# A two-layer decoder trunk on one core: second softmax group's query and key slabs as 512-column products over both parts of x

## The chip, the core and the metric

One NeuronCore of a Trainium2 chip. The metric is the device time of one execution of the whole program in microseconds, the lower the better.

## What is computed

Two layers of a causal decoder trunk for 256 tokens of width 1024, in 32-bit floats. Layer 0 mixes the normed rows by two head groups, A (gated linear recurrence) and B (block-sparse softmax attention); with 256 tokens every past block is selected, so B is plain causal attention with a rotation of the first 32 dimensions of each head:

```python
h = jnp.einsum('bsd,de->bse', xn, w_in)
aq, af, ai, bq, bk, bv, z = jnp.split(h, splits, axis=-1)
ob = moba_attention(rotary(heads(bq), pos, ROPE_DIM, ROPE_THETA),
                    rotary(heads(bk), pos, ROPE_DIM, ROPE_THETA), heads(bv))
y = jnp.concatenate([oa, ob], axis=-1) * jax.nn.silu(z)
x = x + jnp.einsum('bse,ed->bsd', y, w_out)
```

Layer 1 does the same with two other groups (C, D), and cross attention to 256 memory rows follows each layer. Most of the work is products of the 256 rows with weights of 1024 rows.

## The kernel before

**Split numbers.** Products run on TensorE in a reduced 32-bit format. To keep the precision, each operand is split into a rounded part (hi) and a rest (lo), and three of the four products are summed: w_hi·x_hi, w_hi·x_lo, w_lo·x_hi. x stands transposed in `xT`, whose two parts lie side by side.

**Slabs and quarters.** Weights come in 2 MB slabs, in the order of the list `SLABS` (line 50): stage, part, kind, group. Each slab is cut in four quarters of 128x1024. For each quarter, ScalarE (ACT) rounds the raw weights to w_hi (`ahead`, line 518, instruction L530), VectorE (DVE) subtracts to w_lo (`ahead`, line 1124, L1130), and TensorE (PE) multiplies. A ring of four quarters holds w_hi and w_lo, so `ahead(n, q)`, which prepares quarter 4n + q + 3, waits until the quarter four places back has been used (`quarter_used`). The raw slabs alternate between two buffers; SyncE starts a slab's transfer when the slab two places back has been split.

**Kinds.** An F quarter (`quarter_f`, line 1832, L1848 to L1850) makes for each of eight k three matmuls of 256 columns into one half of a PSUM bank; two quarters share a bank. An X quarter (`quarter_x`, line 1854, L1863 to L1866) makes for each k one matmul of 512 columns, w_hi with both parts of x side by side, and one of 256, w_lo with x_hi: it fills a whole bank, and the two halves have to be added afterwards. Before the change only the gate slabs (z) are X. T quarters (line 1872) have the rows of x as the stationary operand.

**Banks and turns.** Four PSUM banks serve all slabs, as two pairs. `TURN` (line 77) counts: a slab of kind F or T takes one turn, one of kind X two (first and second half of its quarters). A turn's pair is its number modulo 2. `take_bank` (line 1826) lets PE into a bank only when the turn two before has released it:

```python
def bank(n, u, half=0):
    return proj[2 * ((TURN[n] + half) % 2) + u]
def take_bank(n, u, half=0):
    before = (TURN[n] + half) // 2
    if before >= 1:
        pe.wait_ge(free_of(n, u, half), before)
```

**Who releases.** For F and T slabs ACT copies the bank out (`copy_bank`, line 589, L591) and releases. For a z half ACT copies the first 256 columns of both banks (`z_half`, line 579, L586), DVE adds the other 256 (`sum_z`, line 1180, L1185) and DVE releases.

**The stage.** Group 1 of B is `stage_b(1)` on each engine (PE line 2123, ACT line 738, DVE line 1485); the order of the work on each is written out by hand. Its slabs before the change, with their turns: z of group 0 (X, turns 13 and 14), q (F, 15), k (F, 16), v (T, 17), z (X, 18 and 19).
- PE: q quarters 0 and 1; the transposes of group 0's probabilities (`turn_probs_b`, L2109); q quarter 2; group 0's values (`out_b`, L2101); q quarter 3; k; v; first z quarter; the scores (L2144, L2146), which wait for `q_ready`, `k_ready` and `y_ready`; the other z quarters.
- ACT: the copies of the transposed probabilities (`turned_probs`, L779); `ahead(q, 0)`; `z_half` for group 0's second z half; the SiLU of z (`silu`, L576, with a table load); then further `ahead` calls between the copies of q and k. `turn_rows_packed` (line 728) copies the 32 rotated rows of each head into `packed` (L735, twice) and the bank into W (L591). `y_high(2)` (L601) rounds the gated output of group 0.
- DVE: `ahead(q, 0)`; `sum_z` for that z half; `ahead`; the gated output of group 0 (`gated_b`, line 1465, L1470); `ahead`; the rotation of q and of k (`rope_moba`, line 1420, L1425 to L1433).

Of the kernel before, what the change touches and what calls it, by code (L numbers as in the profile page):

```python
# [52 lines left out]
for _g in range(2):  # L53
    SLABS += [("B", "q", "F", _g), ("B", "k", "F", _g), ("B", "v", "T", _g), ("B", "z", "X", _g)]
# [36 lines left out]
def hybrid_trunk(nc, I, out):  # L91
    with ExitStack() as ctx:
# [136 lines left out]
        o_rstd = sem("o_rstd")  # L229
        q_rows = sem("q_rows_copied")  # L230
# [89 lines left out]
        def z_sum(n):  # L320

            if SLABS[n][0] == "C":
                return att[:, :, 0:S]
            return zs[:]

# [191 lines left out]
        def _(act):  # L517
# [210 lines left out]
            def turn_rows_packed(n, u, w, s):  # L728

                filled(act, n, u)  # L730
                if w == 0 and u == 0:
                    act.wait_ge(k_ready, SLABS[n][3])
                for h in range(2):
                    a = 64 * u + 32 * h
                    act.activation(packed[a:a + 32, 2 * w, :], bank(n, u)[0:32, S * h:S * h + S], ACT.Copy)  # L735
                copy_bank(n, u, W[:, w, 512 * u:512 * u + 512], s)

            def stage_b(g):
# [7 lines left out]
                turn_rows_packed(q, 0, 0, q_rows)  # L746
                ahead(q, 3)
                if g:
                    y_high(2)
                ahead(k, 0)  # L750
                turn_rows_packed(q, 1, 0, q_rows)
                ahead(k, 1)
                if g == 0:
                    act.preload_act_table_set("natural_log_exp_and_others")
                    rstd_a(1)
                ahead(k, 2)
                turn_rows_packed(k, 0, 1, k_rows)
                ahead(k, 3)
                if g == 0:
                    y_high(1)  # L760
                ahead(v, 0)
                turn_rows_packed(k, 1, 1, k_rows)
                ahead(v, 1)
# [359 lines left out]
        def _(dve):  # L1123
# [55 lines left out]

            def sum_z(n, half):  # L1180
# [5 lines left out]
                dve.drain().then_inc(free_of(n, 0, half), 1)  # L1186
                dve.nop().then_inc(free_of(n, 1, half), 1)
# [247 lines left out]

            def softmax_max(i, h, moba):
# [48 lines left out]
            def stage_b(g):  # L1485
# [8 lines left out]
                if g == 0:  # L1494
                    mem_turned(0)
                ahead(q, 3)
                if g == 0:
                    mem_turned(1)
                if g:
                    gated_b(0)  # L1500
                ahead(k, 0)
                ahead(k, 1)
                if g == 0:
                    gated_a(1)
                ahead(k, 2)
                rope_moba(0, q_rows, q_ready, 2 * g + 2, k, 3)
                ahead(v, 0)
                rope_moba(1, k_rows, k_ready, 2 * g + 2, v, 1)
                ahead(v, 2)
# [311 lines left out]
        def _(pe):  # L1821
# [32 lines left out]
            def quarter_x(n, q):  # L1854
# [7 lines left out]
                for k in range(KC - 1):  # L1862
                    pe.matmul(both, wh[:, k, :], xT[:, :, k, :], start=(k == 0), stop=False)  # L1863
                    pe.matmul(dst[:, 0:S], wl[:, k, :], xT_hi[:, k, :], start=False, stop=False)  # L1864
                pe.matmul(dst[:, 0:S], wl[:, KC - 1, :], xT_hi[:, KC - 1, :], start=False, stop=False)  # L1865
                pe.matmul(both, wh[:, KC - 1, :], xT[:, :, KC - 1, :], start=False, stop=True).then_inc(quarter_used, 1)  # L1866

            def slab_x(n, qs=range(4)):
                for q in qs:
                    quarter_x(n, q)  # L1870
# [252 lines left out]
            def stage_b(g):  # L2123
# [7 lines left out]
                else:  # L2131
                    slab_f(q, [0, 1])
                    turn_probs_b(0)
                    slab_f(q, [2])
                    out_b(0)
                    slab_f(q, [3])
                    slab_f(k)
# [234 lines left out]
```

## Time and profile before

| | us |
|---|---|
| median of 3 runs | 584.78 (584.31 to 584.93) |
| the profiled execution | 585.06 |
| its span, first to last instruction | 583.2 |
| PE busy | 573.4 (98%) |
| DVE busy | 426.0 (73%) |
| ACT busy | 390.6 (67%) |
| mean granted TensorE clock | 0.999 |

Busy time is the union of an engine's instructions. The ends of matmuls are modelled and overlap the next one, so the pace of a stream of matmuls is read from the starts, not from the durations. PEld is TensorE's loading of the stationary operand, which runs beside the matmuls. Idle time of an engine counts only where the chain of waits goes through it.

### The profile page before, as it was taken

How to read it: one execution, taken by the hardware profiler on the slowest of the kernel's cores; microseconds unless marked ns; L12 is line 12 of the kernel's file. 1: busy time of each engine (PE TensorE's matmuls, PEld its weight loads, DVE VectorE, ACT ScalarE, POOL GpSimd, SP SyncE). 2: the span in 40 equal slices, each digit the busy share in tenths (PEclk: the TensorE clock that was granted, in tenths of full speed). 3: DMA queues.
4: the chain of work that ended last, by engine and by line, in shares of the span. 5: the costliest groups of instructions: out<-in, count | busy, mean ns of one | idle time of the engine just before them, and what ended most of it. 6: DMA issues, size and time to landing. Idle time of an engine off the chain costs nothing.

```text
span 583.2 us, 9261 instructions
## 1 busy us (share of the span) xinstructions
PE 573.4 (98%) x3612; PEld 518.5 (89%) x3612; DVE 426.0 (73%) x662; ACT 390.6 (67%) x597; POOL 73.7 (13%) x77
## 2 busy tenths in 40 slices
PE   7999999999999999999999999999999999999995
PEld 6999989899899888889988999999889988888985
DVE  6879779686756874567557865799997974876663
ACT  6863784578458575657666847969759837566754
POOL 4330005026401000100000001102110200100002
PEclk9999999999999999999999999999999999999999
DMA  9757355556824833565345545326544563356201
GB/s 294 242 182 234 92 198 188 175 158 173 238 83 148 286 145 144 178 221 180 145 144 169 193 151 194 121 113 218 215 146 145 162 247 142 112 207 227 97 1 73
DMA packets 51855, 98.86 MB, mean 170 GB/s; under 512 B 1732, under 2 KB 7140, under 8 KB 51812
## 3 DMA queue, kind: packets, MB, share of 16 engines
q1 hardware_dynamic: 50628, 96.95, 49.2%
q0 software_dynamic: 1024, 1.05, 0.7%
q8 instruction: 29, 0.48, 0.3%
q10 hardware_dynamic: 160, 0.27, 0.1%
q14 instruction: 14, 0.11, 0.1%
HBM read 96.16 MB, written 1.05 MB: 167 GB/s over the span
## 4 chain that ended last, share of the span: by engine, by line
PE 97%; DVE 1%; DMA 1%; ACT 0%; issue 0%; SPq 0%; DVEq 0%; ACTq 0%
PE proj L1848 12%; PE proj L1850 11%; PE proj L1849 11%; PE proj L1885 11%; PE proj L1887 11%; PE proj L1886 11%; PE proj L1863 9%; PE proj L1864 5%; PE head L2101 4%; PE proj L1866 1%; PE head L2177 1%; PE head L2284 1%; PE head L1945 1%; DMA x_residual<-in_x_dram 1%; PE proj L1865 1%; PE head L2078 1%
## 5 line engine op out<-in xcount | busy, mean ns | idle before, releaser
L1130 DVE TENSOR_TENSOR w_lo<-raw_weights,w_hi 128x1024 fp32r<-128x1024 f32 x174 | 223.9, 1300 | 99.1 <-ACT w_hi L530 96.5
L530 ACT ACTIVATE w_hi<-raw_weights 128x1024 fp32r<-128x1024 f32 x174 | 182.2, 1056 | 111.5 <-PE proj L1887 49.2
L1848 PE MATMUL proj<-xT,w_hi 128*128 128x256 f32 x496 | 142.4, 287 | 0.0
L1850 PE MATMUL proj<-xT,w_lo 128*128 128x256 f32 x496 | 140.4, 283 | 0.0
L1849 PE MATMUL proj<-xT,w_hi 128*128 128x256 f32 x496 | 140.3, 283 | 0.0
L1848 PEld LDWEIGHTS proj<-xT,w_hi 128*128 128x128 f32 x496 | 95.0, 192 | 0.8 <-DVEq L1186 0.4
L1849 PEld LDWEIGHTS proj<-xT,w_hi 128*128 128x128 f32 x496 | 95.1, 192 | 0.5
L1850 PEld LDWEIGHTS proj<-xT,w_lo 128*128 128x128 f32 x496 | 95.0, 192 | 0.0
L1863 PE MATMUL proj<-xT,w_hi 128*128 128x512 f32 x224 | 81.1, 401 | 0.0
L1885 PE MATMUL proj<-w_hi,y_hi 128*128 128x512 f32 x176 | 69.4, 395 | 0.0
L1887 PE MATMUL proj<-w_lo,y_hi 128*128 128x512 f32 x176 | 68.6, 390 | 0.0
L1886 PE MATMUL proj<-w_hi,y_lo 128*128 128x512 f32 x176 | 68.5, 389 | 0.0
L1864 PE MATMUL proj<-xT,w_lo 128*128 128x256 f32 x224 | 62.7, 280 | 0.0
L1863 PEld LDWEIGHTS proj<-xT,w_hi 128*128 128x128 f32 x224 | 42.1, 188 | 8.8
L1864 PEld LDWEIGHTS proj<-xT,w_lo 128*128 128x128 f32 x224 | 42.3, 189 | 0.8
L443 POOL TENSOR_TENSOR y_lo<-work,y_hi 128x1024 fp32r<-128x1024 f32 x6 | 15.7, 2609 | 193.5 <-ACT y_hi L601 193.5
L1887 PEld LDWEIGHTS proj<-w_lo,y_hi 128*128 128x128 f32 x176 | 33.0, 188 | 7.0
L1886 PEld LDWEIGHTS proj<-w_hi,y_lo 128*128 128x128 f32 x176 | 33.1, 188 | 6.7
L1885 PEld LDWEIGHTS proj<-w_hi,y_hi 128*128 128x128 f32 x176 | 33.1, 188 | 6.7
L1885 PE MATMUL proj<-w_hi,xT 128*128 128x512 f32 x96 | 37.4, 390 | 0.0
L1886 PE MATMUL proj<-w_hi,xT 128*128 128x512 f32 x96 | 37.4, 390 | 0.0
L1887 PE MATMUL proj<-w_lo,xT 128*128 128x512 f32 x96 | 37.3, 389 | 0.0
(313 smaller groups left out, 901.5 us busy)
## 6 DMA issues: line engine op xcount, KB each, us to landing
raw_weights<-in_ev_w_in_dram SPq DMA_DIRECT2D x15, 2048.0 KB, 9.7
raw_weights<-in_od_w_in_dram SPq DMA_DIRECT2D x12, 2048.0 KB, 8.0
raw_weights<-in_ev_w_out_dram SPq DMA_DIRECT2D x4, 2048.0 KB, 7.7
raw_weights<-in_xa_wkv_dram SPq DMA_DIRECT2D x4, 2048.0 KB, 8.3
raw_weights<-in_od_w_out_dram SPq DMA_DIRECT2D x4, 2048.0 KB, 7.7
raw_weights<-in_xa_wq_dram SPq DMA_DIRECT2D x2, 2048.0 KB, 9.0
raw_weights<-in_xa_wo_dram SPq DMA_DIRECT2D x2, 2048.0 KB, 8.4
x_residual<-in_x_dram SPq DMA_DIRECT2D x2, 512.0 KB, 4.1
```

The lines of the kernel that those rows point to most:

```text
L443: pool.tensor_tensor(y_lo[:, 4 * G:4 * G + 4, :], y_src(i), y_hi[:, 4 * G:4 * G + 4, :].bitcast(F32), ALU.subtract).then_inc(y_lo_ready, 1)
L530: act.activation(ring_quarter(w_hi, n, q), raw_quarter(n, q), ACT.Copy).then_inc(hi_ready, 1)
L1130: dve.tensor_tensor(ring_quarter(w_lo, n, q), raw_quarter(n, q), ring_quarter(w_hi, n, q).bitcast(F32), ALU.subtract).then_inc(lo_ready, 1)
L1848: pe.matmul(dst, wh[:, k, :], x_hi[:, k, :], start=(k == 0), stop=False)
L1849: pe.matmul(dst, wh[:, k, :], x_lo[:, k, :], start=False, stop=False)
L1850: last = pe.matmul(dst, wl[:, k, :], x_hi[:, k, :], start=False, stop=(k == KC - 1))
L1863: pe.matmul(both, wh[:, k, :], xT[:, :, k, :], start=(k == 0), stop=False)
L1864: pe.matmul(dst[:, 0:S], wl[:, k, :], xT_hi[:, k, :], start=False, stop=False)
L1885: pe.matmul(dst, x_hi[:, k0 + k, tok], wh[:, k, :], start=first and k == 0, stop=False)
L1886: pe.matmul(dst, x_lo[:, k0 + k, tok], wh[:, k, :], start=False, stop=False)
L1887: last = pe.matmul(dst, x_hi[:, k0 + k, tok], wl[:, k, :], start=False, stop=final and k == 1)
L2101: last = pe.matmul(dst[:, a:a + w], v_sb[:, t, P * h:P * h + P], src, start=(j == 0), stop=(j == len(spans) - 1), skip_group_check=True)
```

## The change

The q and k slabs of B's group 1 become kind X. On PE their eight quarters go through `quarter_x` (which gets arguments for the source of x and for a wait on it, unused here), so each fills a bank. For each of the four halves (two quarters each) ACT copies the first 256 columns of both banks into W (`halves_copied`), DVE adds the other 256 in place and releases the banks (`sum_rows`), and ACT copies the 32 rotated rows of each of two heads from W into `packed` (`packed_rows`). The turns become: q 15 and 16, k 17 and 18, v 19, z 20 and 21. The order of ACT's and DVE's work in `stage_b` is written anew for group 1; PE's order stays. Group 0 stays as it was.

```diff
@@ -51,7 +51,7 @@
 for _g in range(2):
     SLABS += [("A", "f", "F", _g), ("A", "i", "T", _g), ("A", "q", "F", _g), ("A", "z", "X", _g)]
 for _g in range(2):
-    SLABS += [("B", "q", "F", _g), ("B", "k", "F", _g), ("B", "v", "T", _g), ("B", "z", "X", _g)]
+    SLABS += [("B", "q", "FX"[_g], _g), ("B", "k", "FX"[_g], _g), ("B", "v", "T", _g), ("B", "z", "X", _g)]
 SLABS += [("OUT0", (0, 0), "T", 0), ("OUT0", (0, 1), "T", 0), ("OUT0", (1, 0), "T", 0), ("OUT0", (1, 1), "T", 0)]
 SLABS += [("XA0", "k", "F", 0), ("XA0", "q", "F", 0), ("XA0", "v", "T", 0), ("XA0", "o", "W", 0), ("XA1", "k", "F", 0)]
 for _g in range(2):
@@ -227,6 +227,10 @@
         square_split = sem("square_split")
         ms_psum = sem("ms_psum")
         o_rstd = sem("o_rstd")
+        q_halves = sem("q_halves_copied")
+        q_summed = sem("q_summed")
+        k_halves = sem("k_halves_copied")
+        k_summed = sem("k_summed")
         q_rows = sem("q_rows_copied")
         k_rows = sem("k_rows_copied")
         q_ready = sem("q_ready")
@@ -323,6 +327,11 @@
                 return att[:, :, 0:S]
             return zs[:]
 
+        def bank_halves(n, half, w):
+
+            pair = 2 * ((TURN[n] + half) % 2)
+            return proj_banks[:, pair:pair + 2, S * w:S * w + S]
+
         def y_src(i):
 
             if i == 5:
@@ -728,12 +737,24 @@
             def turn_rows_packed(n, u, w, s):
 
                 filled(act, n, u)
-                if w == 0 and u == 0:
-                    act.wait_ge(k_ready, SLABS[n][3])
                 for h in range(2):
                     a = 64 * u + 32 * h
                     act.activation(packed[a:a + 32, 2 * w, :], bank(n, u)[0:32, S * h:S * h + S], ACT.Copy)
                 copy_bank(n, u, W[:, w, 512 * u:512 * u + 512], s)
+
+            def halves_copied(n, half, w, s):
+
+                filled(act, n, 1, half)
+                act.activation(blocks(w)[:, 2 * half:2 * half + 2, :], bank_halves(n, half, 0), ACT.Copy).then_inc(s, 1)
+
+            def packed_rows(half, w, summed, s):
+
+                act.wait_ge(summed, half + 1)
+                if w == 0 and half == 0:
+                    act.wait_ge(k_ready, 1)
+                for h in (2 * half, 2 * half + 1):
+                    last = act.activation(packed[32 * h:32 * h + 32, 2 * w, :], blocks(w)[0:32, h, :], ACT.Copy)
+                last.then_inc(s, 1)
 
             def stage_b(g):
                 q, k, v, z = (slab("B", c, g) for c in "qkvz")
@@ -743,24 +764,38 @@
                 silu(before)
                 ahead(q, 1)
                 ahead(q, 2)
-                turn_rows_packed(q, 0, 0, q_rows)
-                ahead(q, 3)
-                if g:
+                if g:
+                    halves_copied(q, 0, 0, q_halves)
+                    ahead(q, 3)
                     y_high(2)
-                ahead(k, 0)
-                turn_rows_packed(q, 1, 0, q_rows)
-                ahead(k, 1)
-                if g == 0:
+                    packed_rows(0, 0, q_summed, q_rows)
+                    ahead(k, 0)
+                    halves_copied(q, 1, 0, q_halves)
+                    ahead(k, 1)
+                    packed_rows(1, 0, q_summed, q_rows)
+                    ahead(k, 2)
+                    halves_copied(k, 0, 1, k_halves)
+                    ahead(k, 3)
+                    packed_rows(0, 1, k_summed, k_rows)
+                    ahead(v, 0)
+                    halves_copied(k, 1, 1, k_halves)
+                    ahead(v, 1)
+                    packed_rows(1, 1, k_summed, k_rows)
+                else:
+                    turn_rows_packed(q, 0, 0, q_rows)
+                    ahead(q, 3)
+                    ahead(k, 0)
+                    turn_rows_packed(q, 1, 0, q_rows)
+                    ahead(k, 1)
                     act.preload_act_table_set("natural_log_exp_and_others")
                     rstd_a(1)
-                ahead(k, 2)
-                turn_rows_packed(k, 0, 1, k_rows)
-                ahead(k, 3)
-                if g == 0:
+                    ahead(k, 2)
+                    turn_rows_packed(k, 0, 1, k_rows)
+                    ahead(k, 3)
                     y_high(1)
-                ahead(v, 0)
-                turn_rows_packed(k, 1, 1, k_rows)
-                ahead(v, 1)
+                    ahead(v, 0)
+                    turn_rows_packed(k, 1, 1, k_rows)
+                    ahead(v, 1)
                 ahead(v, 2)
                 ahead(v, 3)
                 ahead(z, 0)
@@ -1177,14 +1212,18 @@
                 dve.nop().then_inc(free_of(n, 1, half), 1)
 
 
+            def halves_freed(n, half):
+
+                dve.drain().then_inc(free_of(n, 0, half), 1)
+                dve.nop().then_inc(free_of(n, 1, half), 1)
+
             def sum_z(n, half):
 
                 dve.wait_ge(z_copied, 2 * Z_SLABS.index(n) + half + 1)
                 pair = 2 * ((TURN[n] + half) % 2)
                 rows = z_sum(n)[:, 2 * half:2 * half + 2, :]
                 dve.tensor_tensor(rows, proj_banks[:, pair:pair + 2, S:2 * S], rows, ALU.add).then_inc(z_summed, 1)
-                dve.drain().then_inc(free_of(n, 0, half), 1)
-                dve.nop().then_inc(free_of(n, 1, half), 1)
+                halves_freed(n, half)
 
 
             dve.memset(v_sb[:, 0, 0:P], 1.0)
@@ -1433,6 +1472,13 @@
                     last = dve.tensor_tensor(blocks(w)[0:32, h, :], x[a:a + 32, :], y[a:a + 32, :], ALU.add)
                 last.then_inc(done, 1)
 
+            def sum_rows(n, half, w, copied, summed):
+
+                dve.wait_ge(copied, half + 1)
+                rows = blocks(w)[:, 2 * half:2 * half + 2, :]
+                dve.tensor_tensor(rows, bank_halves(n, half, 1), rows, ALU.add).then_inc(summed, 1)
+                halves_freed(n, half)
+
             def softmax_max(i, h, moba):
 
                 dve.wait_ge(scores, i)
@@ -1491,22 +1537,32 @@
                     dve.drain()
                 ahead(q, 1)
                 ahead(q, 2)
-                if g == 0:
+                if g:
+                    sum_rows(q, 0, 0, q_halves, q_summed)
+                    ahead(q, 3)
+                    gated_b(0)
+                    ahead(k, 0)
+                    sum_rows(q, 1, 0, q_halves, q_summed)
+                    ahead(k, 1)
+                    ahead(k, 2)
+                    sum_rows(k, 0, 1, k_halves, k_summed)
+                    rope_moba(0, q_rows, q_ready, 4, k, 3)
+                    ahead(v, 0)
+                    sum_rows(k, 1, 1, k_halves, k_summed)
+                    ahead(v, 1)
+                    rope_moba(1, k_rows, k_ready, 4, v, 2)
+                else:
                     mem_turned(0)
-                ahead(q, 3)
-                if g == 0:
+                    ahead(q, 3)
                     mem_turned(1)
-                if g:
-                    gated_b(0)
-                ahead(k, 0)
-                ahead(k, 1)
-                if g == 0:
+                    ahead(k, 0)
+                    ahead(k, 1)
                     gated_a(1)
-                ahead(k, 2)
-                rope_moba(0, q_rows, q_ready, 2 * g + 2, k, 3)
-                ahead(v, 0)
-                rope_moba(1, k_rows, k_ready, 2 * g + 2, v, 1)
-                ahead(v, 2)
+                    ahead(k, 2)
+                    rope_moba(0, q_rows, q_ready, 2, k, 3)
+                    ahead(v, 0)
+                    rope_moba(1, k_rows, k_ready, 2, v, 1)
+                    ahead(v, 2)
                 ahead(v, 3)
                 ahead(z, 0)
                 dve.wait_ge(y_lo_ready, 2 + g)
@@ -1851,7 +1907,7 @@
                 if ks[-1] == KC - 1:
                     last.then_inc(quarter_used, 1)
 
-            def quarter_x(n, q):
+            def quarter_x(n, q, x=xT, norm=None):
 
                 u, half = q % 2, q // 2
                 take_bank(n, u, half)
@@ -1860,14 +1916,18 @@
                 both = dst.rearrange("p (w t) -> p w t", w=2)
                 wh, wl = ring_quarter(w_hi, n, q), ring_quarter(w_lo, n, q)
                 for k in range(KC - 1):
-                    pe.matmul(both, wh[:, k, :], xT[:, :, k, :], start=(k == 0), stop=False)
-                    pe.matmul(dst[:, 0:S], wl[:, k, :], xT_hi[:, k, :], start=False, stop=False)
-                pe.matmul(dst[:, 0:S], wl[:, KC - 1, :], xT_hi[:, KC - 1, :], start=False, stop=False)
-                pe.matmul(both, wh[:, KC - 1, :], xT[:, :, KC - 1, :], start=False, stop=True).then_inc(quarter_used, 1)
-
-            def slab_x(n, qs=range(4)):
+                    if norm is not None:
+                        pe.wait_ge(xT_lo_ready, KC * norm + k + 1)
+                    pe.matmul(both, wh[:, k, :], x[:, :, k, :], start=(k == 0), stop=False)
+                    pe.matmul(dst[:, 0:S], wl[:, k, :], x[:, 0, k, :], start=False, stop=False)
+                if norm is not None:
+                    pe.wait_ge(xT_lo_ready, KC * norm + KC)
+                pe.matmul(dst[:, 0:S], wl[:, KC - 1, :], x[:, 0, KC - 1, :], start=False, stop=False)
+                pe.matmul(both, wh[:, KC - 1, :], x[:, :, KC - 1, :], start=False, stop=True).then_inc(quarter_used, 1)
+
+            def slab_x(n, qs=range(4), x=xT, norm=None):
                 for q in qs:
-                    quarter_x(n, q)
+                    quarter_x(n, q, x, norm if q == 0 else None)
 
             def quarter_t(n, q, x_hi, x_lo, k0, half=0, start=True, stop=True):
 
@@ -2129,12 +2189,12 @@
                     slab_f(k)
                     slab_t(v)
                 else:
-                    slab_f(q, [0, 1])
+                    slab_x(q, [0, 1])
                     turn_probs_b(0)
-                    slab_f(q, [2])
+                    slab_x(q, [2])
                     out_b(0)
-                    slab_f(q, [3])
-                    slab_f(k)
+                    slab_x(q, [3])
+                    slab_x(k)
                     slab_t(v)
                 slab_x(z, [0])
                 pe.wait_ge(q_ready, g + 1)
```

## Rows read from the trace of the kernel before

**Rows 1.** The page: busy time, share of the span and instructions of each engine.
```profile
PE 573.4 (98%) x3612; PEld 518.5 (89%) x3612; DVE 426.0 (73%) x662; ACT 390.6 (67%) x597; POOL 73.7 (13%) x77
...
PE 97%; DVE 1%; DMA 1%; ACT 0%; issue 0%; SPq 0%; DVEq 0%; ACTq 0%
```

**Rows 2.** PE's two longest waits of four: for whom, us in total, times, longest.
```profile
PE head L1964 <- DVE shared_rows L1211: 1.8, 2, 1.2
PE proj L1952 <- DVEq L1191: 1.2, 1, 1.2
```

**Rows 3.** Busy time by stretch: from:to, length, PE, PEld, DVE, ACT, POOL, clock, DMA.
```profile
177.47:191.94 14.47, 14.47 (x124) 14.47 (x122) 10.70 (x12) 11.18 (x17) 2.41 (x1) 1.00 0.56 173
```

**Rows 4.** PE in order of time: start, us, line, operation; where each piece of the stage starts.
```profile
159.35 0.40 PE L1863 MATMUL proj<-xT,w_hi 128*128 128x512 f32 x1
...
164.99 0.28 PE L1848 MATMUL proj<-xT,w_hi 128*128 128x256 f32 x1
...
170.75 1.47 PE L2109 MATMUL head<-ident,work 128*128 128x128 f32 x12
171.97 0.36 PE L1848 MATMUL proj<-xT,w_hi 128*128 128x256 f32 x1
...
174.93 2.78 PE L2101 MATMUL head<-work,v_rows 128*128 128x256 f32 x16
177.47 0.36 PE L1848 MATMUL proj<-xT,w_hi 128*128 128x256 f32 x1
...
191.94 0.40 PE L1885 MATMUL proj<-w_hi,xT 128*128 128x512 f32 x1
...
205.66 0.38 PE L2144 MATMUL head<-work 128*128 128x128 f32 x2
```

**Rows 5.** PE in order of time: an X quarter right behind the values of another stage.
```profile
433.23 0.47 PE L1863 MATMUL proj<-xT,w_hi 128*128 128x512 f32 x1
...
436.09 0.28 PE L1848 MATMUL proj<-xT,w_hi 128*128 128x256 f32 x1
```

**Rows 6.** ACT in order of time; in brackets its idle time before, and the releaser.
```profile
171.27 1.64 ACT L779 ACTIVATE work<-head 128x384 f32<-128x384 f32 x4 [6.39 <-PE head L2109]
172.77 1.08 ACT L530 ACTIVATE w_hi<-raw_weights 128x1024 fp32r<-128x1024 f32 x1
173.72 0.62 ACT L586 ACTIVATE z_silu<-proj 128x512 f32<-128x512 f32 x1
...
178.61 0.74 ACT L735 ACTIVATE dmask<-proj 32x256 f32<-32x256 f32 x2
...
183.62 1.06 ACT L601 ACTIVATE y_hi<-work 128x1024 fp32r<-128x1024 f32 x1 [2.49 <-DVE work L1470]
```

**Rows 7.** DVE in order of time, same stretch.
```profile
173.88 1.23 DVE L1130 TENSOR_TENSOR w_lo<-raw_weights,w_hi 128x1024 fp32r<-128x1024 f32 x1 [5.16 <-ACT w_hi L530]
175.03 0.68 DVE L1185 TENSOR_TENSOR z_silu<-proj,z_silu 128x512 f32<-128x512 f32 x1
177.78 2.36 DVE L1130 TENSOR_TENSOR w_lo<-raw_weights,w_hi 128x1024 fp32r<-128x1024 f32 x2 [2.07 <-ACT w_hi L530]
...
182.31 1.28 DVE L1470 TENSOR_TENSOR work<-head,z_silu 128x512 f32<-128x512 f32 x2
...
199.53 1.70 DVE L1433 TENSOR_TENSOR work<-dmask 32x256 f32<-32x256 f32 x4
```

**Rows 8.** DVE and weight loads at the one place where PE waited for a sum's release.
```profile
384.82 0.68 DVE L1185 TENSOR_TENSOR att<-proj,att 128x512 f32<-128x512 f32 x1
...
385.61 0.19 PEld L1848 LDWEIGHTS proj<-xT,w_hi 128*128 128x128 f32 x1 [0.36 <-DVEq L1186]
```

**Rows 9.** PE's last matmul, then busy time by stretch behind it: length, PE, clock, DMA.
```profile
577.00 0.28 PE L1907 MATMUL head<-w_lo,y_hi 128*128 128x256 f32 x1
...
581.50:582.00 0.50, 0.00 (x0) 0.80 1.01 385
582.00:582.50 0.50, 0.00 (x0) 0.50 0.62 226
```

## The prediction

> **What bounds the kernel now.** The page comes first: PE is busy for 573.4 of 583.2 us, and 97% of the chain that ended last lies on PE [rows 1]. The list of PE's waits comes next: the two longest of its four entries make 3.0 us, and the longest single wait is 1.2 us [rows 2]; all lie in the first 11 us or the last 27. In the stage of the change PE has no idle time at all: 14.47 us busy in a stretch of 14.47 us, beside DVE with 10.70 and ACT with 11.18 [rows 3]. So two things can change the time: the pace of the stream of matmuls, and any moment in which PE has to wait. What PE loses here it can't make up later, as it has no slack later either. I therefore read PE's start times of this stage [rows 4], then those of ACT and DVE beside them [rows 6, 7], and ask of each PE piece whether its bank and its weights are there.
>
> **The change on PE.** An F quarter streams 24 x 256 = 6144 columns, an X quarter 8 x (512 + 256) = 6144. No column is saved. What is saved is matmuls: 24 against 16. The first two q quarters took 170.75 - 164.99 = 5.76 us, 2.88 each; the two z quarters ahead of them took 164.99 - 159.35 = 5.64 us, 2.82 each [rows 4]. That is 0.06 us per quarter, or some 7.5 ns for each of the 8 matmuls that go. The Trainium skill, "TensorE: Matmul & The Clock Gate", section on the back-to-back issue gap, gives a warm matmul a fixed 2.5 ns beyond its columns. By it, as an estimate, 64 matmuls fewer would save 0.16 us where the rows give 0.5, and the sum below would be some 0.3 us higher; the rows decide.
>
> Two quarters follow other work and start slower. F took 174.93 - 171.97 = 2.96 us behind the transposes and 2.95 at 177.47 (back from the k quarters) [rows 4]; an X quarter behind the same kind of values took 436.09 - 433.23 = 2.86 [rows 5]. I take 2.86 for both; bounds are 2.82, and 3.0 if X starts no better than F. So the saving is 0.12 for q 0 and 1, 0.10 for q 2, 0.09 for q 3, 4 x 0.06 for k: 0.55 us, if nothing waits.
>
> **The bank that q's third quarter needs.** Here the change adds a wait. As F, q has one turn, 15, on the pair that the first half of z of group 0 (turn 13) left long before. As X it has two, and q quarters 2 and 3 take turn 16: the pair of turn 14, the second half of that z. Before, the first to need that pair was k at about 180.4 us. Now it is q quarter 2, right behind the transposes. Who releases it? DVE, behind the sum L1185 at 175.03, which ends at 175.71 [rows 7]. That sum can't be early, because both engines come to it late: ACT first copies the transposed probabilities, from 171.27, and these need PE's transposes, which stand behind q quarters 0 and 1; then it rounds one quarter (172.77), then copies the z half (173.72) [rows 6]; DVE splits that quarter from 173.88 and then adds [rows 7]. Nothing in this order is changed.
>
> Worked out on PE's clock: the transposes start 0.12 earlier, at 170.63, and take 171.97 - 170.75 = 1.22, so PE is ready for q quarter 2 at 171.85. ACT's and DVE's chain hangs on the transposes and moves by the same 0.12: the sum ends at 175.59. From a sum's end to the start of PE behind it took 385.61 - 385.50 = 0.11 us at the one place where PE waited for it [rows 8]. So quarter 2 starts at 175.70, and PE stands for 3.85 us. Bounds: DVE is idle before this chain (5.16 us before its first piece) and ACT too (6.39) [rows 6, 7], so there is nothing before it to move it either way; with one 0.1 more or less at each of its hand-offs I keep 3.5 to 4.2.
>
> **The rest of the stage, piece by piece.** Quarter 2 ends at 178.56; the values take 177.47 - 174.93 = 2.54, to 181.10; q quarter 3 ends at 183.96; four k quarters of 2.82 end at 195.24, where v starts. Before, v started at 191.94 [rows 4]. That is +3.30 us, which is 3.85 - 0.55.
>
> **What is added beside PE.** DVE gets four sums of the shape of L1185, 0.68 each and 0.24 until its next instruction, 3.7 us; ACT's copies come out even (one of 0.6 and two of 0.37 per half, as now; the packed ones read W instead of PSUM, 0.3 to 0.5 each) [rows 6, 7]. SyncE starts the same transfers, POOL does the same. What covers the sums is the slack of each hand-off, which I follow:
> - k quarter 0 needs the pair of q's first half. ACT copies it from about 178.5, where its row copies stood, DVE adds when its two splits of 177.78 + 2.36 are done (minus 0.12): 179.9 to 180.6. PE comes at 183.96. Slack 3.3 us, which the stall itself has given: without it PE would have come at about 180.1.
> - k quarter 2 needs q's second half, at 183.96 + 5.64 = 189.6. The chain: DVE's next split 180.85 to 182.1, the gated output 1.28 to 183.3, ACT's `y_high` 1.06 to 184.4, packed copies to 185.0, rounding k quarter 3 to 186.0 (it needs q quarter 3 used, 183.96), DVE's split to 187.3, the sum to 187.9. Slack 1.7. It is the tightest; its cost if wrong is a rival below.
> - v needs k's first half at 195.24; by the same counting the sum ends at 192.6. Slack 2.6.
> - The scores need `k_ready`. Now the rotation ends at 201.23 against 205.66, slack 4.4 [rows 4, 7]. After, DVE's two last sums and the later k push it to about 205.3, and PE comes at 195.24 + 13.72 = 208.96. Slack 3.7.
> - ACT's wait on `quarter_used` of q quarter 2 (178.56) for rounding k quarter 2 is met just when ACT gets there (179.0).
> Behind the scores everything is as before, 3.3 us later.
>
> **The sum.** 585.06 for the profiled execution + 3.30 = 588.4. The median of the runs is 584.78, 0.28 lower, so I predict 588.1 us. A measurement of this kernel can tell about 0.2%, 1.2 us, from no change.
>
> **Rivals.**
> *The pair is free in time*, so that the change gives just what its matmuls save: 584.78 - 0.55 = 584.2, within 0.2%. It decides at 171.74: if the z sum ends before that, PE doesn't wait. For it speaks that PE never waited for this pair before, and that both ACT and DVE idle for over 5 us ahead [rows 6, 7]; against it that their order is fixed by hand and the copy stands behind the transposes' copies. It would need me to have misread the turns. No more than 0.55 us can be won in any case, as the columns are the same. Chance 0.04, with the case that some work on PE hides the wait.
>
> *The hand-off of q's second half is late too.* The chain of seven pieces across ACT and DVE above has 1.7 us of slack; if each of its five changes of engine costs 0.3 us or more beyond the row before, or something queues in it, k quarter 2 waits. Price up to 1.5 us: 589.6. For it speaks that in the stage both engines are 74 and 77% busy before the sums come in [rows 3]; against it that the pieces before follow each other with 0.03 us, as `y_high` at 183.62 behind the gated output that ended at 183.59 [rows 6, 7]. Chance 0.06.
>
> *The clock falls in the stall.* Behind PE's last matmul, over at 577.3, the granted clock fell to its lower level (0.50, 1.2 GHz) between 581.5 and 582.0, some 4.5 us later; in the longest idle stretch ahead of other matmuls, 1.2 us, it did not [rows 2, 9]. From the last transpose's end (about 172.1) PE stands for 3.6 us: nearer to the 4.5. At the lower level a quarter of 2.82 us takes up to twice that, so each quarter spent there costs up to 2.8: with one, 588.1 + 2.8 = 590.9. No row shows matmuls at the lower level, so this is a bound and not a measured price. The Trainium skill, same page, section "Why this matters for your kernels", warns that idle gaps between bursts of matmuls throw TensorE back to half rate; by that rule the change costs more than the stall. Chance 0.11.
>
> **How the numbers follow.** The forecast, one stall of 3.5 to 4.2 us less 0.4 to 0.6, has 0.79: 587.6 to 588.6, with the spread of runs 587.3 to 588.9. The range takes in the late second hand-off to 589.6, and a short spell at the lower clock: 587.0 to 590.0. It leaves out the rest of the clock case and the case without a stall. Faster by over 0.2% (below 583.6) is not reached even by the full saving: 0.01. Within 0.2%: 0.03. Slower: 0.96.
>
> **What would show it.** PE's waits would have a new first entry, the first matmul or weight load of `quarter_x` behind DVE's release, one time, 3.5 to 4 us, starting near 172; the clock in that stretch at 1.00; v's first matmul near 195.2; X quarters at 2.82 us; no wait of PE at k quarter 0 or 2 or at the scores. I am wrong if there is no such wait, if a second of over 0.5 us stands in the stage, or if the granted clock falls under 1.00 behind it.

## The result, and the profile after

The changed kernel takes 589.26 us (589.04 to 590.12), the kernel before, timed with it, 584.40 (584.22 to 584.93). The ratio is 1.0076, interval 1.0062 to 1.0090: 0.76% slower, some 4.4 us. The prediction said 588.1, in a range of 587.0 to 590.0. The profiled execution has a span of 587.4 us and a mean granted clock of 0.995 (before 583.2 and 0.999).

The page of the changed kernel, its busy times and the share of engines in the chain that ended last, beside [rows 1]:

```profile
PE 574.3 (98%) x3548; PEld 516.1 (88%) x3548; DVE 427.3 (73%) x666; ACT 391.0 (67%) x597; POOL 73.4 (12%) x77
...
PE 96%; DMA 1%; DVE 1%; ACT 1%; issue 0%; SPq 0%; DVEq 0%; ACTq 0%
```

PE has 64 matmuls fewer and is busy a little longer. Its list of waits (who for whom, us in total, times, longest) has a new first entry, beside [rows 2]:

```profile
PE proj L1921 <- DVEq L1217: 3.6, 1, 3.6
...
PE proj L2012 <- DVEq L1230: 1.2, 1, 1.2
```

L1921 is the 512-column product of `quarter_x`, L1217 the drain in `halves_freed` behind a sum. PE in order of time (start, us, line, idle before) shows where it stands, beside [rows 4]:

```profile
164.73 0.40 PE L1921 MATMUL proj<-xT,w_hi 128*128 128x512 f32 x1
...
170.37 1.47 PE L2169 MATMUL head<-ident,work 128*128 128x128 f32 x12
175.43 0.79 PE L1921 MATMUL proj<-xT,w_hi 128*128 128x512 f32 x1 [3.59 <-DVEq L1217]
...
179.84 2.78 PE L2161 MATMUL head<-work,v_rows 128*128 128x256 f32 x16
182.37 0.47 PE L1921 MATMUL proj<-xT,w_hi 128*128 128x512 f32 x1
...
185.23 0.40 PE L1921 MATMUL proj<-xT,w_hi 128*128 128x512 f32 x1
...
196.48 0.40 PE L1945 MATMUL proj<-w_hi,xT 128*128 128x512 f32 x1
...
210.19 0.38 PE L2204 MATMUL head<-work 128*128 128x128 f32 x2
```

From the start of q to the start of v it is 196.48 - 164.73 = 31.75 us; before it was 191.94 - 164.99 = 26.95 [rows 4]. The stage is 4.80 us longer. The wait ahead of q quarter 2 is there. The quarter behind it takes 179.84 - 175.43 = 4.41 us, though, where an undisturbed one takes 2.8 to 2.9. The busy time by stretch (length, PE busy with its count, granted clock, DMA share, GB/s) tells why:

```profile
174.50:175.00 0.50, 0.00 (x0) 1.00 0.00 0
175.00:175.50 0.50, 0.07 (x1) 0.82 0.00 0
175.50:178.00 2.50, 2.50 (x8) 0.50 0.83 229
...
178.50:179.00 0.50, 0.50 (x3) 0.76 1.01 287
179.00:180.00 1.00, 1.00 (x7) 1.00 0.90 254
```

The granted clock fell to its lower level, 1.2 GHz, at the end of the time in which PE stood idle (its stand, for short) and came back near 178.7. Two losses add up: the wait, and most of a quarter at half rate. The releasing chain on ACT and DVE is the one of [rows 6, 7], 0.38 us earlier:

```profile
172.40 1.08 ACT L539 ACTIVATE w_hi<-raw_weights 128x1024 fp32r<-128x1024 f32 x1
173.34 0.62 ACT L595 ACTIVATE z_silu<-proj 128x512 f32<-128x512 f32 x1
```

```profile
174.65 0.68 DVE L1225 TENSOR_TENSOR z_silu<-proj,z_silu 128x512 f32<-128x512 f32 x1
...
179.68 0.68 DVE L1479 TENSOR_TENSOR work<-proj,work 128x512 f32<-128x512 f32 x1
...
188.13 0.68 DVE L1479 TENSOR_TENSOR work<-proj,work 128x512 f32<-128x512 f32 x1
```

The z sum ends at 175.33, PE starts at 175.43.

### The profile page after: what moved, and what is told of

It is laid out like the page before. It is cut to its first block, busy times and chain, and to the rows that moved or that the text cites. A ratio compares the mean times of both kernels' runs of the same rounds, so it can differ in the third digit from the quotient of the medians.

```text
span 587.4 us, 9140 instructions
## 1 busy us (share of the span) xinstructions
PE 574.3 (98%) x3548; PEld 516.1 (88%) x3548; DVE 427.3 (73%) x666; ACT 391.0 (67%) x597; POOL 73.4 (12%) x77
## 4 chain that ended last, share of the span: by engine, by line
PE 96%; DMA 1%; DVE 1%; ACT 1%; issue 0%; SPq 0%; DVEq 0%; ACTq 0%
PE proj L1921 11%; PE proj L1945 11%; PE proj L1946 11%; PE proj L1947 10%; PE proj L1904 10%; PE proj L1906 10%; PE proj L1905 10%; PE proj L1922 6%; PE head L2161 4%; PE proj L1926 2%; PE head L2237 1%; PE head L2344 1%; DMA raw_weights<-in_ev_w_in_dram 1%; PE head L2005 1%; PE proj L1925 1%; PE head L2138 1%
## 5 line engine op out<-in xcount | busy, mean ns | idle before, releaser
L1904 PE MATMUL proj<-xT,w_hi 128*128 128x256 f32 x432 | 124.1, 287 | 0.0
L1905 PE MATMUL proj<-xT,w_hi 128*128 128x256 f32 x432 | 122.2, 283 | 0.0
L1921 PE MATMUL proj<-xT,w_hi 128*128 128x512 f32 x280 | 102.8, 405 | 3.6 <-DVEq L1217 3.6
L1904 PEld LDWEIGHTS proj<-xT,w_hi 128*128 128x128 f32 x432 | 82.8, 192 | 0.8 <-DVEq L1217 0.4
L1905 PEld LDWEIGHTS proj<-xT,w_hi 128*128 128x128 f32 x432 | 82.8, 192 | 0.4
L1921 PEld LDWEIGHTS proj<-xT,w_hi 128*128 128x128 f32 x280 | 53.4, 191 | 15.0 <-DVEq L1217 3.8
```

The source lines that it names most:

```text
L1904: pe.matmul(dst, wh[:, k, :], x_hi[:, k, :], start=(k == 0), stop=False)
L1905: pe.matmul(dst, wh[:, k, :], x_lo[:, k, :], start=False, stop=False)
L1921: pe.matmul(both, wh[:, k, :], x[:, :, k, :], start=(k == 0), stop=False)
```

## The experiments

My theory after the result: PE stands for the pair of banks that the sum of z's second half releases; the clock falls because PE stands; the 512-column form by itself only saves. Rivals: the wait hangs on something else; the slow quarter has another cause; the X form costs something that the stall covers. As the start of the program varies by some tenths of a microsecond, and in some executions by 2 to 3 us, I compare the stage in the traces, from the first transpose to the first matmul of v: 191.94 - 170.75 = 21.19 us before, 196.48 - 170.37 = 26.11 with the change.

**The z half summed earlier.** From the changed kernel, ACT's copy and DVE's sum of that half move ahead into idle time. The diffs here are shortened; their headers name the place.

```diff
@@ scalar
             stage_b(0)
+            z_half(slab("B", "z", 0), 1)
             for h in range(4):
                 turned_probs(h + 1, h, 384)
@@ scalar, stage_b
-                z_half(before, 1)
+                if g == 0:
+                    z_half(before, 1)
@@ vector, stage_b
+                if g:
+                    sum_z(slab("B", "z", 0), 1)
                 ahead(q, 0)
-                sum_z(slab("B", "z", 0) if g else slab("A", "z", 1), 1)
                 if g == 0:
+                    sum_z(slab("A", "z", 1), 1)
```

> Only the second half of group 0's z is copied (ACT) and summed (DVE) earlier: ahead of the copies of the transposed probabilities and ahead of the split of q quarter 3, in a stretch where both engines idle. Theory 1 (PE stands for the pair of banks that this sum releases, and the clock falls because it stands): PE's wait of 3.6 us ahead of q quarter 2 is gone, the granted clock stays at 1.00, q quarter 2 takes about 2.86 us, not 4.41. The second hand-off then turns late: k quarter 2 is wanted at about 185.5 and q's second half is summed at about 187.2, so a new wait of 1.2 to 2.2 us, and one of 0 to 0.5 at k quarter 0. Time 585.0 to 586.6 against 584.4 before and 589.3 with the change. Rival (the wait hangs on something else, as the weights of q quarter 2 or the transposes' banks): the wait stays at 3 us or more and the time at 589. Second rival (enough slack everywhere): 583.9.

Measured: 586.45 us (ratio 1.0036, 1.0019 to 1.0052). PE in order of time, from its trace:

```profile
170.06 1.47 PE L2173 MATMUL head<-ident,work 128*128 128x128 f32 x12
171.29 0.47 PE L1925 MATMUL proj<-xT,w_hi 128*128 128x512 f32 x1
...
187.58 0.50 PE L1925 MATMUL proj<-xT,w_hi 128*128 128x512 f32 x1 [2.03 <-DVEq L1219]
...
193.33 0.40 PE L1949 MATMUL proj<-w_hi,xT 128*128 128x512 f32 x1
```

The wait ahead of q quarter 2 is gone, the clock of the stage is 1.00, and q quarter 2 takes 174.15 - 171.29 = 2.86 us. The late second hand-off came as expected, 2.03 us ahead of k quarter 2. On DVE, in the same trace:

```profile
185.17 1.71 DVE L1167 TENSOR_TENSOR w_lo<-raw_weights,w_hi 128x1024 fp32r<-128x1024 f32 x1 [2.95 <-ACT w_hi L539]
186.80 0.68 DVE L1481 TENSOR_TENSOR work<-proj,work 128x512 f32<-128x512 f32 x1
```

The split in front of the sum takes 1.71 us, not 1.23. POOL's subtraction for the gated output runs from 183.39 to 185.79, over the first 0.62 us of it. The stage is 23.27 us, 2.84 shorter than with the change. So moving one sum removes the first wait and lays the second one bare, which the first had covered.

**The values first.** PE's order alone.

```diff
                     turn_probs_b(0)
-                    slab_x(q, [2])
                     out_b(0)
-                    slab_x(q, [3])
+                    slab_x(q, [2, 3])
```

> Only PE's order differs from the changed kernel: group 0's values (2.54 us of PE work that needs only the copied probabilities) come right behind the transposes, and q quarters 2 and 3 follow. Theory 1: PE waits about 1.0 us for the copies (171.6 to 172.6), works till 175.1, waits about 0.3 us for the bank, and the clock stays at 1.00, as no stretch without matmuls is over 1.2 us. k quarter 0 would start 4.1 us earlier than with the change; k quarter 2 then waits about 1 us for the sum of q's second half. Time 585.0 to 586.5. Rival (the clock falls for another reason than the long stand, as the kind of products): clock below 1.00 here too and 1.5 us more, 586.7 to 588.

Measured: 587.36 us (1.0044, 1.0027 to 1.0060). That is above the 586.5 I gave and inside the rival's 586.7 to 588. Three of its six executions lie between 586.30 and 586.53, three between 588.19 and 589.08. The profiled one is among the latter and shows the lower clock in the first 20 us of the program and not in this stage, so its trace speaks against the rival; that the other two slow ones are slow for the same reason is likely, not shown. PE from its trace:

```profile
172.07 1.47 PE L2169 MATMUL head<-ident,work 128*128 128x128 f32 x12
174.38 2.85 PE L2161 MATMUL head<-work,v_rows 128*128 128x256 f32 x16 [0.84 <-ACT work L814]
...
190.09 0.50 PE L1921 MATMUL proj<-xT,w_hi 128*128 128x512 f32 x1 [1.43 <-DVEq L1217]
...
195.81 0.39 PE L1945 MATMUL proj<-w_hi,xT 128*128 128x512 f32 x1
```

The stand of 3.59 has become one of 0.84, the clock of the stage is 1.00, and k quarter 2 waits 1.43 us. The stage takes 23.74 us, 2.37 shorter than with the change. Only a part of that is the filling itself: an execution of the changed kernel in which the clock stayed up (below) has a stage of 24.71, so 0.97 comes from the order and the other 1.40 from the clock.

**The wait filled, twelve and four products.** Products into an idle bank that nobody reads, ahead of q quarter 2; the first kernel has twelve of them, the second four.

```diff
                     turn_probs_b(0)
+                    pe.wait_ge(probsT_ready, 4)
+                    split_ready(q, 2)
+                    for j in range(12):
+                        pe.matmul(head[3][:].rearrange("p (w t) -> p w t", w=2),
+                                  ring_quarter(w_hi, q, 2)[:, j % KC, :],
+                                  xT[:, :, j % KC, :], start=True, stop=True)
                     slab_x(q, [2])
```

> Twelve products of 512 columns that nobody reads are added on PE into an idle bank while it would stand (from the moment when the probabilities are copied, about 172.5, for 2.8 us). Nothing else differs from the changed kernel; the release of the bank comes when it came, near 175.4. Theory 1: the granted clock stays at 1.00 and q quarter 2 takes 2.8 to 2.95 us and not 4.41, so the time falls by 1.4 to 1.6 us, to 587.7 to 587.9. Rival (the slow quarter isn't due to the standing still): time 589.3 and a clock below 1.00 as before.

> As the run with twelve unread products in PE's wait, with four of them (0.9 us) right behind the copies of the probabilities; so PE stands about 0.8 us, works 0.9 to 1.0, and stands about 1.9 us till the bank is released. Theory 1 (one long stand brings the clock down, short ones do not): clock 1.00, time as with twelve, 587.7 to 588.0. Rival (the share of idle time counts, however it is split): the clock falls below 1.00 here too and the time is 588.8 to 589.5.

Measured: twelve 588.21 us (1.0059, 1.0042 to 1.0076; four executions, two at 587.8), above the 587.7 to 587.9 expected; four 587.42 (1.0053, 1.0033 to 1.0073), below the 587.7 to 588.0. The intervals of both overlap that of the change, so the evidence is in the traces. The clock is 1.00 through the stage in both. With twelve, PE's pieces are:

```profile
171.28 1.47 PE L2169 MATMUL head<-ident,work 128*128 128x128 f32 x12
173.49 3.03 PE L2197 MATMUL head<-xT,w_hi 128*128 128x512 f32 x12 [0.75 <-ACT work L814]
176.36 0.47 PE L1921 MATMUL proj<-xT,w_hi 128*128 128x512 f32 x1
...
195.87 0.40 PE L1945 MATMUL proj<-w_hi,xT 128*128 128x512 f32 x1
```

The stage is 195.87 - 171.28 = 24.59 us, 1.52 shorter than with the change, though PE does 2.8 us more work. With four:

```profile
169.90 1.47 PE L2169 MATMUL head<-ident,work 128*128 128x128 f32 x12
172.12 1.19 PE L2197 MATMUL head<-xT,w_hi 128*128 128x512 f32 x4 [0.74 <-ACT work L814]
174.97 0.50 PE L1921 MATMUL proj<-xT,w_hi 128*128 128x512 f32 x1 [1.66 <-DVEq L1217]
177.66 0.40 PE L1926 MATMUL proj<-xT,w_hi 128*128 128x512 f32 x1
```

Two stands of 0.74 and 1.66 us didn't bring the clock down here, where one of 3.59 did, each in the one trace there is. The z sum ends when it did, 4.95 to 4.97 us behind the first transpose (4.96 with the change). So the slow quarter doesn't come with the X products or with the late release: it is a price that a long stand can have. The next run shows that it need not.

**The changed kernel again**, unchanged.

> The changed kernel itself once more, on the same chip as the others: 589.0 to 589.6, with PE's wait of 3.6 us and the lower clock behind it. If the time or the clock differed much, the fall of the clock would be a matter of luck and the comparisons above would need more runs.

Measured: 589.03 us (1.0077, 1.0053 to 1.0102); 587.69, 588.78, 589.27 and 591.38. It ran on the chip of the four products, the wait alone and the z sum moved in the kernel before, not on that of the other experiments. The median is the expected one, the lower clock isn't there in the profiled execution, the 587.69, and this is the most telling trace of the study:

```profile
170.23 1.47 PE L2169 MATMUL head<-ident,work 128*128 128x128 f32 x12
175.29 0.50 PE L1921 MATMUL proj<-xT,w_hi 128*128 128x512 f32 x1 [3.59 <-DVEq L1217]
...
178.22 2.01 PE L2161 MATMUL head<-work,v_rows 128*128 128x256 f32 x11
...
194.94 0.40 PE L1945 MATMUL proj<-w_hi,xT 128*128 128x512 f32 x1
```

```profile
175.00:177.00 2.00, 1.71 (x9) 1.00 0.66 183
```

The same stand of 3.59 us, but the clock stayed at 1.00, and q quarter 2 took 178.22 - 175.29 = 2.93 us. The stage is 24.71 us, 1.40 shorter than in the other trace, and the span is 585.8, 1.6 shorter. Whether the clock falls in a stand of 3.6 us is thus a matter of the execution. The twelve unread products bring the stage to 24.59, so against this execution they gain next to nothing: what they buy is the clock. Of the ten executions of this program, this one has a mean clock of 0.998, the other nine 0.993 to 0.996. The mean alone doesn't say where it was lost, as a fall in the first 20 us of the program lowers it just as much (0.995 in the profiled execution of the values first).

**The wait alone.** From the kernel before, with all quarters F.

```diff
                     turn_probs_b(0)
+                    pe.wait_ge(bank_free[0], 8)
                     slab_f(q, [2])
```

> The kernel before with one thing added: ahead of q quarter 2 of group 1 PE waits for the release of the pair of z's second half, as the changed kernel has to. All quarters stay F. Theory 1 (the whole loss is this wait and the clock that falls in it, and the conversion itself only saves some 0.5 us): PE stands 3.6 to 3.9 us, q quarter 2 runs partly at the lower clock and takes 4.3 to 4.7 us instead of 2.96; the time is 0.5 us above that of the change, 589.4 to 590.2. Rival (the X form has a cost of its own): clearly under the change, 588.8 or less.

Measured: 590.58 us (1.0111, 1.0083 to 1.0138), from 589.78, 589.84, 591.32 and 593.98; the profiled one is the longest.

```profile
173.41 1.47 PE L2109 MATMUL head<-ident,work 128*128 128x128 f32 x12
178.48 0.58 PE L1848 MATMUL proj<-xT,w_hi 128*128 128x256 f32 x1 [3.59 <-DVEq L1186]
...
183.77 2.95 PE L2101 MATMUL head<-work,v_rows 128*128 128x256 f32 x16
```

```profile
177.00:178.00 1.00, 0.00 (x0) 0.64 0.00 0
...
178.50:183.00 4.50, 4.50 (x21) 0.50 0.88 242
...
184.00:185.00 1.00, 1.00 (x6) 0.95 1.05 401
```

The same wait, to a hundredth, and here a longer spell at the lower clock, from about 177.3 to 184: quarter 2 takes 5.29 us instead of 2.96. The median is above the 590.2 that I gave. The two shorter executions lie 5.2 and 5.3 us above their kernel before, some 0.5 more than the change costs in most of its own. So the conversion adds no loss of its own; the wait and what it does to the clock are enough. The spread of four executions is too wide to read the 0.5 as a measurement; the reordered version, below, shows more firmly what the form does.

**The z sum moved in the kernel before.** The edit of the first experiment, with all quarters F.

> The kernel before with only the z half of group 0 copied and summed earlier, as in the two kernels with the z sum first. All quarters F. PE never waited there, so theory 1 expects no change: within 0.3 us of before. Rival (the reordered kernel is faster than before because of the earlier z sum and not because of the fewer matmuls): 583.5 to 583.9.

Measured: 584.83 us (1.0000, 0.9990 to 1.0010). No effect, as before no piece of PE waited for that sum.

**The reordered version.** The first experiment, and in it both engines come to q's halves earlier: ACT copies the first ahead of the SiLU and the second ahead of `y_high`, DVE adds the first ahead of its next splits and the second right behind the gated output.

```diff
@@ scalar, stage_b, group 1
+                    halves_copied(q, 0, 0, q_halves)
                 silu(before)
                 ahead(q, 1)
                 ahead(q, 2)
-                    halves_copied(q, 0, 0, q_halves)
                     ahead(q, 3)
-                    y_high(2)
                     packed_rows(0, 0, q_summed, q_rows)
-                    ahead(k, 0)
                     halves_copied(q, 1, 0, q_halves)
+                    y_high(2)
+                    ahead(k, 0)
@@ vector, stage_b, group 1
+                    sum_rows(q, 0, 0, q_halves, q_summed)
                 ahead(q, 1)
                 ahead(q, 2)
-                    sum_rows(q, 0, 0, q_halves, q_summed)
                     ahead(q, 3)
                     gated_b(0)
-                    ahead(k, 0)
                     sum_rows(q, 1, 0, q_halves, q_summed)
+                    ahead(k, 0)
```

> As the run with the z sum first, and in addition ACT copies the first half of q ahead of the SiLU and the second half ahead of rounding the gated output, and DVE adds the first half ahead of its next splits and the second half right behind the gated output. Theory 1: all releases come before PE wants them (first half near 175 against 179.9, second near 182.5 against 185.5, k's first near 189 against 191), PE never waits in the stage, and only the saving of the fewer matmuls is left, 0.4 to 0.6 us: 583.8 to 584.0, against 584.4 before. Rival (the conversion has a cost of its own that the stall covers, as PSUM or SBUF contention of the 512-column products with the copies): 584.4 or more without a wait of PE.

Measured: 583.55 us (583.40 to 586.57, twelve executions) against 584.65: 0.9985, interval 0.9973 to 0.9997. The median is below the 583.8 to 584.0 expected. It is the fastest kernel of the study, by a margin just clear of noise, and all of PE's waits in its trace lie in the first microseconds of the program:

```profile
172.71 1.47 PE L2175 MATMUL head<-ident,work 128*128 128x128 f32 x12
176.56 0.40 PE L1932 MATMUL proj<-xT,w_hi 128*128 128x512 f32 x1
176.79 2.78 PE L2167 MATMUL head<-work,v_rows 128*128 128x256 f32 x16
...
193.44 0.40 PE L1951 MATMUL proj<-w_hi,xT 128*128 128x512 f32 x1
```

```profile
176.99 0.68 DVE L1482 TENSOR_TENSOR work<-proj,work 128x512 f32<-128x512 f32 x1
...
184.35 0.68 DVE L1482 TENSOR_TENSOR work<-proj,work 128x512 f32<-128x512 f32 x1
```

The stage is 20.73 us, 0.46 shorter than before, and with 0.12 for the two quarters ahead of it that is 0.58: the saving of fewer matmuls, as worked out. q's second half is summed by 185.03, and k quarter 2 starts at 187.8. The ratio says 0.9 us, with an interval from 0.2 to 1.6; the 0.3 beyond the 0.58 is what the traces show at the very end of the program, next.

**Twelve empty instructions on DVE, in the kernel before.** Behind the stage the converted kernels are 0.3 us shorter as well. In the last softmax, near 558 us (567 in the wait alone), four traces with F quarters have a gap on DVE and a wait of PE. The start of PE's score products there and that of the transposes behind them lie 3.13 to 3.15 us apart in these four, and 2.81 to 2.82 in seven traces with X quarters.

```diff
+                if g:
+                    for _ in range(12):
+                        dve.nop()
                 ahead(q, 0)
```

> The kernel before with twelve empty instructions on DVE in a stretch where it idles for 5 us (ahead of its first split in group 1's stage); nothing else. In the traces every kernel with F quarters there (before, the wait alone, the z sum moved in the kernel before) has a gap of 0.23 us on DVE ahead of a reciprocal in the last softmax and a wait of PE of 0.2 behind it; the kernels with X quarters, which have more DVE instructions ahead of it, have that gap elsewhere and PE's pieces there take 2.82 us and not 3.15. Theory: the gap's place hangs on the count of DVE's instructions, so with twelve more it moves and PE's wait is gone: 0.3 us less than before. Rival: the place hangs on the work of that stage and nothing moves: as before, with PE's wait of 0.2.

Measured: 584.36 us (0.9999, 0.9990 to 1.0008). My theory falls: the gap stayed, and so did PE's wait.

```profile
557.76 0.17 DVE L1456 RECIPROCAL stats<-stats 128x2 f32<-128x2 f32 x1 [0.22 <-issue]
```

What moves it stays open. That all seven traces with X quarters lack it and all four with F have it is shown; that the conversion causes it is not.

## Why the prediction was right or wrong

**The cause and the place were right.** q quarter 2 needs the pair of z's second half, and PE stood for it 3.59 us by the list of waits; from being ready (170.37 + 1.22 = 171.59) to the start at 175.43 it is 3.84, forecast 3.85. Moving only that sum took the wait away, adding only that wait to the kernel before brought the loss.

**The pieces.** q quarters 0 and 1: 5.64 us, forecast 5.64. The values: 2.53, forecast 2.54. q quarter 3 behind them: 2.86, forecast 2.86. Four k quarters: 11.25, forecast 11.28. v and the first z quarter: 13.71, forecast 13.72. The hand-off from the sum's end to PE: 0.10, forecast 0.11. The saving of the form, 0.55 forecast, is 0.58 in the reordered version. The fixed 2.5 ns per matmul of the Trainium skill ("TensorE: Matmul & The Clock Gate", back-to-back issue gap) would have made it 0.16, and here the trace is the one that holds: 7.5 ns.

**The step that failed** is "the clock in that stretch at 1.00", and with it the order of the cases. I gave a fall of the clock 0.11, since in the one idle stretch of the trace in which it fell it took 4.5 us behind PE's last matmul [rows 9], and the stand is 3.6. It fell in the profiled execution, by the prediction's own list a sign of being wrong. Seven of the ten executions lie between 588.8 and 589.4, as the profiled one does (589.21), so it most likely fell in those; for the two longer ones a slow start is as good a reason. In its price, up to 2.8 us, I had only a bound: quarter 2 took 4.41 us and not 2.86, 1.55 more, in the trace of the change, and 2.33 more in the one of the wait alone. The sum with it, 3.30 + 1.55 = 4.85, is the 4.80 of the stage. The measured 589.26 lies outside the 587.3 to 588.9 that the forecast itself has with its spread. It is inside the range only because that was widened for the two rivals. Without the fall, the execution at 587.69 us is the forecast: its stage is 24.71 - 21.19 = 3.52 longer, less 0.12 for the two quarters ahead, 3.40 against 3.30. The rule in the same page of the Trainium skill, in "Why this matters for your kernels", that idle gaps between bursts throw PE to half rate, was the better guide here; the traces agree with it in two of the three that have the stand of 3.59 us (the change, the wait alone) and not in the third.

**The hand-offs that I found with slack.** k quarter 0 and k quarter 2 did not wait in the changed kernel, as said. The chain in front of k quarter 2 was longer than my count, though: its sum ended at 188.81, forecast 187.9 in a program that started 0.26 us later. Two things in it I had not counted: ACT's rounding of k quarter 2 waited for q quarter 2, which the lower clock had made late (it ran from 180.03, forecast 179.0), and DVE's split took 1.68 us beside POOL. The kernel before had shown the second already: its split at 185.66 took 2.59 us beside POOL. PE came later as well, at 190.8, so 2.0 us of slack were left; in the execution in which the clock stayed up the sum ended at 188.15 and PE came at 189.3, so it was 1.15, where I had counted 1.7. The first experiment shows what the chain costs without the stall: 2.03 us.

**The end of the program** came 0.3 us earlier than with F quarters, which nothing in the prediction held, and whose cause is open. 4.80 - 0.33 = 4.47, which is what the ratio says, 4.4.

## What to carry to other kernels

A buffer that one stage takes in two turns instead of one reaches back to an earlier owner: before a conversion of this kind, list for every piece which turn it takes and who released it last, not only whether the consumer's own new steps are hidden. Where the bounding engine has to wait as long as here, 3.6 us, look at the clock behind it, and fill or split the wait, even with useless work: with unread products in it the quarter behind ran at full rate and the stage was 1.5 us shorter than where the clock had fallen, and 0.1 than where it had not. And don't stop at the first wait taken away; here it covered a second one of 2 us, and only with both gone did the saving of 0.6 us show.

## What I had not expected of the hardware

- The same program with the same stand of 3.59 us had its clock at 1.00 in one execution and at 0.50 for over 3 us in another. The low spell began 3.5 us behind the last transposes in the trace of the change and lasted till 178.7; in the wait alone it began about 2.4 us behind them and lasted some 6.8 us. At the end of the kernel before it began 4.5 us behind the last matmul. A stand of 2.03 us left it at 1.00 in the one trace that has it.
- Shorter stands are no guarantee. In the start of the program PE stood 0.74, 0.62 and 1.93 us in the values first, with 1 us of transposes between them, and the clock fell right behind the last, from 11.0 to 14.4 us; with twelve products it stood 0.39 and 1.90 us there, and the clock stayed at 1.00. In the profiled executions of the values first, the reordered version and the wait alone, the mean clock of the first 20 us was 0.91, and PE's waits for x there 1.9 to 2.5 us instead of 0.6 before. So the profiled execution of the reordered version took 586.18 us, where the median of its twelve is 583.55.
- Subtractions of 128x1024 on DVE took 1.68 to 1.72 us instead of 1.23 when the first 0.6 us of them fell into one of POOL's, and 2.59 us when the first 1.5 did (the kernel before, the reordered version). In all of them DVE ended 1.08 to 1.09 us behind POOL's end, as if it had hardly moved till then.
